# Where the row loads of the second and third expert pair are requested in a routed MoE on one core

## The chip, the cores and the metric

One core of one Trainium2 chip runs the whole program. The metric is the device time of one execution in microseconds (us). The kernel before took 1014.53 us in the median of 3 runs (1013.32 to 1015.21).

## The reference, cut to what matters

Two layers (DEPTH = 2) follow one another. Each mixes the tokens, attends to a memory, and ends with a mixture of experts on 256 tokens of width 1024. The experts' part is what the change touches:

```python
g_logits = t @ w_rg                       # 4 groups; the best one is taken
e_in = e_logits of that group             # its 4 experts; the best two are taken
e_w = softmax(top 2 of e_in) * g_w
...
hg = einsum('nd,edf->nef', t, w_gate)     # 16 experts, 1024 -> 512
hu = einsum('nd,edf->nef', t, w_up)
act = silu(hg) * hu * gates
y = einsum('nef,efd->nd', act, w_down)    # 512 -> 1024
```

So each token goes to two of sixteen experts.

## The kernel before, in words

All is float32. Each engine has a program of its own, written out by hand, and semaphores tie them together.

**Weights.** SyncE (SP) requests all weight units of 2 MB in halves of 1 MB (L520), in a fixed order, into a ring of 7 slots and some buffers that have become free (one more in the first layer, three in the second). Before it requests a unit it waits until its slot's tenant has been read. For expert units this is the semaphore slots_read, which ScalarE (ACT) counts up: it waits for TensorE's count r_jobs and then adds one (units_read, L1336 to L1339). For the first pair of experts there are counts named half (the first half of gate's two units has been read), gate, up, and one at the end of the pair. The last pair's up and down units come in quarters (L561), the two experts' quarters in turn.

**Sorting tokens.** The router gives each token two slots of a table by_slot in HBM (64 rows for each of 16 experts). GpSimd (POOL) sends the normalised tokens there with four indirect transfers (L1498); their landing is counted by r_sent. The first pair's rows do not come from the table: TensorE gathers them on the chip (L975) and starts at once. The rows of pair p from 1 on are loaded back from by_slot by ACT, 512 KB for each pair, with load_rows(p) (L1334), into one of two halves of the buffer rot. For pairs 1 and 2 these two requests stand in ACT's program behind the first exponential of pair 0 (L1347). From pair 3 on the request stands three pairs ahead.

**One pair of experts on TensorE (PE).** gate_up(p) (L1040) multiplies the rows by gate and then by up; VectorE (DVE) makes silu(gate)*up from ACT's exponential (L2011 to L2017). turned(p) then has two parts: the transposes of that product (L1089), and the transposes of the next pair's rows (rows_transposes, L1064), which wait for r_loaded of those rows. In the first layer's pair 0 the rows' transposes come first (rows_first, L179). In the second layer's pair 0 they come after the product's. Behind both stand the gate weights' transposes (L1097), the down product (L1110), and, in the first layer's pairs 0 to 4, a piece of the next layer's keys and values (L628, L630), for which ACT requests 2 MB units (L1252) on its own queue. The results are added back to the tokens by to_tokens (L1071) and DVE (L1993).

The order on ACT around the change is that of the code: wait for half, add to slots_read; wait for gate, add to slots_read; wait for r_sent; exponential; two requests; wait for up, add to slots_read; and so on.

Of the kernel before, what the change touches and what calls it, by code (L numbers as in the profile page):

```python
# [19 lines left out]
M = T // P  # L20
# [194 lines left out]
def trunk(nc, x_in, mem_in, pos_in, inv_in, gains_in, og_in, w_mix, w_router, w_experts, nf_in, out):  # L215
    ctx = ExitStack()
    with ctx:
# [117 lines left out]
        def per_layer(name):  # L335
            return [sem(f"{name}{l}") for l in range(DEPTH)]
# [20 lines left out]
        r_sent = per_layer("r_sent")  # L357
# [822 lines left out]
        def _(act):  # L1180
# [48 lines left out]
            for L in range(DEPTH):  # L1229
# [24 lines left out]
                def next_kv(j, b):  # L1254
                    empty_kv(L + 1, j, b)
                    if j % 2 and j < 7:
                        load_kv((j + 1) // 2)
# [75 lines left out]
                def load_rows(p):  # L1333
                    act.dma_start(rows[p % 2], by_slot[p * P:(p + 1) * P, :]).then_inc(r_loaded[L][p % 2], 16)  # L1334

                def units_read(p, name):  # L1336

                    act.wait_ge(r_jobs[L], ROUTED[L][p, name])
                    act.sem_inc(slots_read, 1)  # L1339

                def routed(p):
                    if p == 0:
                        units_read(p, "half")
                    units_read(p, "gate")
                    if p == 0:
                        act.wait_ge(r_sent[L], 16 * 2 * M)
                    nc.scalar.activation(rexp_of[L], banks[2][:, :], ACT.Exp, scale=-1.0).then_inc(r_gexp[L], 1)  # L1347
                    if p == 0:
                        for q in (1, 2):
                            load_rows(q)  # L1350
                    units_read(p, "up")
                    for half in range(2):
                        act.wait_ge(r_jobs[L], ROUTED[L][p, f"act{half}"])
                        nc.scalar.activation(ractT_of[L][:, 2 * half:2 * half + 2, :], banks[ACT_BANK[half]][:, 0:2 * P].rearrange("p (c t) -> p c t", c=2),
                                             ACT.Copy).then_inc(r_evac[L], 1)
                    act.wait_ge(r_jobs[L], ROUTED[L][p, "weights"])
                    nc.scalar.activation(gatedT, banks[7][:, 0:M * P].rearrange("p (m t) -> p m t", m=M), ACT.Copy).then_inc(r_evac[L], 1)
                    if p + 3 < PAIRS:
                        load_rows(p + 3)
                    for n in range(2):  # L1360
                        act.wait_ge(r_jobs[L], ROUTED[L][p, f"down{n}"])
                        nc.scalar.activation(yrows[:, n * W:(n + 1) * W], banks[5 + n][:, :], ACT.Copy).then_inc(r_evac[L], 1)  # L1362
                    act.sem_inc(slots_read, 1)
                    if L + 1 < DEPTH and ROUTER_KV + p < LOOP_KV:
                        next_kv(ROUTER_KV + p, banks[0])
# [13 lines left out]
                def dense_last():  # L1379
                    if L + 1 < DEPTH:  # L1380
                        for j in range(ROUTER_KV, LOOP_KV):
                            next_kv(j, banks[j])

                either_way(act, L, routed, dense, None, None, None, dense_last)

            squares_of_sums(DEPTH - 1)
# [732 lines left out]
```

## Time and profile before

| what | value |
|---|---|
| median of 3 runs | 1014.53 us |
| the profiled execution | 1015.3 us |
| its span, first to last instruction | 1013.4 us |
| its mean granted TensorE clock | 0.993 |
| PE busy | 988.4 us, 98% |
| DVE busy | 485.1 us, 48% |
| ACT busy | 136.5 us, 13% |
| POOL busy | 98.4 us, 10% |
| loads of ring slots by SP | 64.9% of 16 DMA engines' span |

Times in the profile count from the first instruction; the execution is 1.9 us longer than the span. In the lists of instructions the columns are: start (us), duration (us), engine, line, operation, output<-inputs, count of merged instructions, and in brackets the idle time of the engine before it and what ended it. An engine name with a q is its sequencer, which issues DMAs. The first layer's expert part lies at about 305 to 555 us, the second layer's at about 790 to 1006 us.

### The profile page before, as it was taken

What the parts mean: (1) busy time and instruction counts of PE and PEld (TensorE: products, weight loads), DVE (VectorE), ACT (ScalarE), POOL (GpSimd) and SP (SyncE); (2) the same over time, 40 slices, a digit from 0 to 9 for tenths busy, and PEclk for the clock granted to TensorE, in tenths of its full rate; (3) what the DMA queues carried; (4) which work ended last, traced back from release to release, by engine and by line L of the source; (5) the groups of instructions that cost most, each with busy time, mean ns of one, the idle gap of its engine ahead of it and who ended that gap; (6) DMA issues with size and microseconds to landing.
All of it is one profiled execution on the core that took longest, in us unless ns stands there. A gap on an engine that the chain in (4) does not pass through costs nothing.

```text
span 1013.4 us, 11694 instructions
## 1 busy us (share of the span) xinstructions
PE 988.4 (98%) x4744; PEld 532.2 (53%) x4744; DVE 485.1 (48%) x845; ACT 136.5 (13%) x323; POOL 98.4 (10%) x123
## 2 busy tenths in 40 slices
PE   8999999999998999999999999999999899999996
PEld 7658445669574453333333854465974333333332
DVE  2534386766554224422444636776656434444334
ACT  3211001412011010101112000041020101111111
POOL 3051032000020000000000513210000100000000
PEclk9999999999999999999999999999999999999999
DMA  9973101864289999999999420077385899999995
GB/s 356 425 310 122 45 1 48 372 249 163 88 309 377 397 424 419 420 423 420 421 422 420 180 84 1 1 288 284 133 316 210 340 403 421 420 420 421 420 417 200
DMA packets 44828, 293.61 MB, mean 290 GB/s; under 512 B 5472, under 2 KB 5728, under 8 KB 13024
## 3 DMA queue, kind: packets, MB, share of 16 engines
q1 hardware_dynamic: 38000, 266.36, 64.9%
q10 hardware_dynamic: 5616, 22.24, 5.6%
q0 software_dynamic: 1152, 4.19, 1.1%
q8 instruction: 40, 0.66, 0.3%
q14 instruction: 20, 0.16, 0.0%
HBM read 283.33 MB, written 9.44 MB: 289 GB/s over the span
## 4 chain that ended last, share of the span: by engine, by line
PE 94%; DMA 2%; DVE 2%; POOL 1%; issue 1%; ACT 0%; POOLq 0%; DVEq 0%; ACTq 0%
PE bank L1040 20%; PE bank L1110 11%; PE bank L598 8%; PE bank L1071 6%; PE bank L628 6%; PE bank L813 6%; PE bank L630 5%; PE bank L608 5%; PE bank L867 5%; PE bank L931 5%; PE bank L701 5%; PE bank L588 2%; DMA rot<-by_slot 2%; PE bank L901 1%; PE bank L885 1%; PE bank L1064 1%
## 5 line engine op out<-in xcount | busy, mean ns | idle before, releaser
L1040 PE MATMUL bank<-ring,hT 128*64 128x512 f32 x704 | 195.0, 593 | 0.0
L1040 PEld LDWEIGHTS bank<-ring,hT 128*64 128x64 f32 x704 | 62.3, 137 | 87.4 <-issue 87.4
L598 PE MATMUL bank<-ring,hT 128*128 128x512 f32 x192 | 85.6, 599 | 0.0
L1993 DVE TENSOR_TENSOR x<-bank,x 128x512 f32<-128x512 f32 x64 | 44.3, 692 | 51.1 <-PE bank L1071 51.1
L2011 DVE TENSOR_SCALAR xs<-xs 128x512 f32<-128x512 f32 x8 | 3.4, 427 | 124.2 <-ACT xs L1347 124.1
L1071 PE MATMUL bank<-PT 128*128 128x512 f32 x128 | 59.2, 605 | 0.0
L1110 PE MATMUL bank<-ring,Vx 128*64 128x512 f32 x160 | 57.9, 603 | 0.0
L598 PEld LDWEIGHTS bank<-ring,hT 128*128 128x128 f32 x192 | 35.5, 190 | 40.7 <-issue 40.2
L1110 PE MATMUL bank<-ring,xs 128*64 128x512 f32 x224 | 56.7, 595 | 0.0
L608 PE MATMUL bank<-hT,ring 128*128 128x256 f32 x256 | 55.7, 379 | 0.8 <-DVE hT L1622 0.8
L813 PE MATMUL bank<-ring,hT 128*128 128x512 f32 x128 | 56.3, 595 | 0.1
L608 PEld LDWEIGHTS bank<-hT,ring 128*128 128x128 f32 x256 | 48.6, 190 | 8.0 <-issue 1.4
L1040 PE MATMUL bank<-work,hT 128*64 128x512 f32 x112 | 49.3, 593 | 0.0
L1415 POOL TENSOR_TENSOR sm<-sm 128x1 f32<-128x1 f32 x4 | 1.0, 242 | 462.8 <-ACT rot L1225 462.8
L1071 PEld LDWEIGHTS bank<-PT 128*128 128x128 f32 x128 | 23.0, 189 | 35.9 <-issue 34.2
L813 PEld LDWEIGHTS bank<-ring,hT 128*128 128x128 f32 x128 | 23.8, 190 | 28.6 <-issue 28.1
L2011 DVE TENSOR_SCALAR Vx<-Vx 128x512 f32<-128x512 f32 x8 | 3.4, 427 | 72.7 <-ACT Vx L1347 72.7
L1622 DVE TENSOR_TENSOR hT<-bank,gains 128x512 f32<-128x512 f32 x24 | 15.4, 685 | 35.5 <-PE bank L588 35.5
L1362 ACT ACTIVATE PT<-bank 128x512 f32<-128x512 f32 x32 | 19.1, 597 | 97.9 <-PE bank L1110 97.9
L1040 PEld LDWEIGHTS bank<-work,hT 128*64 128x64 f32 x112 | 15.2, 137 | 32.0 <-issue 32.0
L1477 POOL TENSOR_TENSOR work<-work 128x256 f32<-128x256 f32 x28 | 20.7, 741 | 115.6 <-PE bank L736 100.7
L1110 PEld LDWEIGHTS bank<-ring,xs 128*64 128x64 f32 x224 | 17.5, 137 | 25.0 <-issue 25.0
(302 smaller groups left out, 1550.0 us busy)
## 6 DMA issues: line engine op xcount, KB each, us to landing
ring<-in_w_experts SPq DMA_DIRECT2D x146, 1024.0 KB, 14.0
ring<-in_w_mix SPq DMA_DIRECT2D x60, 1024.0 KB, 14.1
work<-in_w_experts SPq DMA_DIRECT2D x20, 1024.0 KB, 11.2
late<-in_w_experts SPq DMA_DIRECT2D x10, 1024.0 KB, 13.2
late<-in_w_mix ACTq DMA_DIRECT2D x4, 2048.0 KB, 10.2
keys<-in_w_experts SPq DMA_DIRECT2D x8, 1024.0 KB, 16.4
rot<-by_slot ACTq DMA_DIRECT2D x14, 512.0 KB, 8.0
by_slot<-late ACTq DMA_DIRECT2D x1, 4096.0 KB, 37.9
```

Of the source, the lines that this page charges most:

```text
L598: last = nc.tensor.matmul(b[:, :], lhs[:, c, m * P:(m + 1) * P], w[:, c, :], start=(c == 0), stop=(c == C - 1))
L608: last = nc.tensor.matmul(b[:, k * T:(k + 1) * T], w[:, c, (n2 + k) * P:(n2 + k + 1) * P], rhs[:, c, :], start=(c == 0), stop=(c == C - 1))
L628: last = nc.tensor.matmul(b[:, k * T:(k + 1) * T], w[:, c, n:n + P], memory[:, c, :], start=(c == 0), stop=(c == C - 1))
L630: last = nc.tensor.matmul(b[:, :], memory[:, c, (j % 2) * P:(j % 2 + 1) * P], w[:, c, :], start=(c == 0), stop=(c == C - 1))
L701: last = nc.tensor.matmul(b[:, :], rows_at[:, c, :], weights[:, c, :], start=(c == 0), stop=(c == 3))
L813: last = nc.tensor.matmul(held[name[1:], n, m][:, :], hT[:, c, m * P:(m + 1) * P], w[:, c, :], start=(c == 0), stop=(c == C - 1))
L867: last = nc.tensor.matmul(b[:, n * P:(n + 1) * P], weights[:, c, n * P:(n + 1) * P], rows_at[:, c, :], start=(name not in ONTO and n == 0 ...
L931: last = nc.tensor.matmul(b[:, :], rows_at[:, c, :], weights[:, c, :], start=(name not in ONTO and c == 0), stop=(c == 3), skip_group_chec ...
L1040: last = nc.tensor.matmul(banks[2 + g][b2 * CAP:(b2 + 1) * CAP, :], rows_T_of(p)[:, c, b2 * CAP:(b2 + 1) * CAP], w, start=(c == 0), stop=( ...
L1071: routed_job(nc.tensor.matmul(banks[OUT_BANK[n][m]][:, :], gatedT[:, m, :], yrows[:, n * W:(n + 1) * W], start=True, stop=True))
L1110: last = nc.tensor.matmul(banks[5 + n][b2 * CAP:(b2 + 1) * CAP, :], ractT_of[L][:, c, b2 * CAP:(b2 + 1) * CAP], w, start=(c == 0), stop=(c ...
L1993: V.tensor_tensor(xv, banks[OUT_BANK[n][m]][:, :], xv, ALU.add).then_inc(r_added[L], 1)
```

## The change

In ACT's routed(p), for pair 0 alone, the wait for r_sent and the request for pair 1's rows stand between the count half and the count gate. The request for pair 2's rows stays behind the exponential.

```diff
@@ -1341,13 +1341,12 @@
                 def routed(p):
                     if p == 0:
                         units_read(p, "half")
+                        act.wait_ge(r_sent[L], 16 * 2 * M)
+                        load_rows(1)
                     units_read(p, "gate")
-                    if p == 0:
-                        act.wait_ge(r_sent[L], 16 * 2 * M)
                     nc.scalar.activation(rexp_of[L], banks[2][:, :], ACT.Exp, scale=-1.0).then_inc(r_gexp[L], 1)
                     if p == 0:
-                        for q in (1, 2):
-                            load_rows(q)
+                        load_rows(2)
                     units_read(p, "up")
```

ACT's program in the first layer, from the end of the branch that is not taken to the end of pair 0, before (r_jobs is TensorE's count, r_sent the landing of GpSimd's sends, rot the buffer for rows, xs the exponential's place in this layer; the additions to slots_read are not rows of their own):

```order
L496 UNCONDITIONAL_BRANCH
L1347 ACTIVATE xs<-bank 128x512 [waits r_jobs0,r_sent0]
L1334 DMA rot<-by_slot 128x1024 x2
L1354 ACTIVATE xs<-bank 128x256 [waits r_jobs0] x2
L1357 ACTIVATE PT<-bank 128x256 [waits r_jobs0]
L1334 DMA rot<-by_slot 128x1024
L1362 ACTIVATE PT<-bank 128x512 [waits r_jobs0] x2
```

The same place of the changed kernel, whose lines behind the edit have numbers lower by one:

```order
L496 UNCONDITIONAL_BRANCH
L1334 DMA rot<-by_slot 128x1024 [waits r_jobs0,r_sent0]
L1347 ACTIVATE xs<-bank 128x512 [waits r_jobs0]
L1334 DMA rot<-by_slot 128x1024
L1353 ACTIVATE xs<-bank 128x256 [waits r_jobs0] x2
L1356 ACTIVATE PT<-bank 128x256 [waits r_jobs0]
L1334 DMA rot<-by_slot 128x1024
```

One request has moved ahead of the exponential, and the wait for r_sent has moved with it.

ACT's program in the second layer at the same place (Vx is the exponential's place there), before:

```order
L1347 ACTIVATE Vx<-bank 128x512 [waits r_jobs1,r_sent1]
L1334 DMA rot<-by_slot 128x1024 x2
L1354 ACTIVATE Vx<-bank 128x256 [waits r_jobs1] x2
L1357 ACTIVATE PT<-bank 128x256 [waits r_jobs1]
L1334 DMA rot<-by_slot 128x1024
```

And changed:

```order
L1334 DMA rot<-by_slot 128x1024 [waits r_jobs1,r_sent1]
L1347 ACTIVATE Vx<-bank 128x512 [waits r_jobs1]
L1334 DMA rot<-by_slot 128x1024
L1353 ACTIVATE Vx<-bank 128x256 [waits r_jobs1] x2
L1356 ACTIVATE PT<-bank 128x256 [waits r_jobs1]
```

The move is the same one. No instruction of PE, DVE, POOL or SP has moved.

## Rows read from the trace of the kernel before

**Rows 1.** The page: busy times, and the shares of the chain.

```profile
PE 988.4 (98%) x4744; PEld 532.2 (53%) x4744; DVE 485.1 (48%) x845; ACT 136.5 (13%) x323; POOL 98.4 (10%) x123
...
PE 94%; DMA 2%; DVE 2%; POOL 1%; issue 1%; ACT 0%; POOLq 0%; DVEq 0%; ACTq 0%
```

**Rows 2.** The chain of waits, first layer: start us, us, what.

```profile
306.91 7.10 PE bank L1040 x32
...
314.15 9.22 DMA rot<-by_slot
...
323.41 1.09 PE bank L1064 x8
324.50 0.44 PE bank L1089 x4
...
325.20 7.09 PE bank L1110 x32
332.28 7.10 PE bank L628 x32
```

**Rows 3.** The list of instructions in order of time, first layer.

```profile
302.14 0.95 POOL L1498 DMA_INDIRECT by_slot<-xs,wsm  x1 [0.31 <-issue]
...
314.12 0.60 ACT L1347 ACTIVATE xs<-bank 128x512 f32<-128x512 f32 x1 [8.37 <-PE bank L1040]
314.15 1.01 ACTq L1334 DMA_DIRECT2D rot<-by_slot  x2
...
320.97 0.76 DVE L2017 TENSOR_TENSOR xs<-bank,xs 128x256 f32<-128x256 f32 x2 [1.16 <-PE bank L1040]
...
323.41 1.09 PE L1064 MATMUL bank<-ident,rot 128*128 128x128 f32 x8 [2.55 <-DMA rot<-by_slot]
```

**Rows 4.** The line L520 from 310 to 312 us, then L1334 from 310 to 316 us.

```profile
L520 SPq DMA_DIRECT2D ring<-in_w_experts x2: 328/906/1484, 310.6 to 311.0; - x2
...
L1334 ACTq DMA_DIRECT2D rot<-by_slot x2: 347/490/632, 314.1 to 314.5; - x2
...
DMA to landing us min/median/max: 9.2/10.9/12.6
```

**Rows 5.** The chain of waits, second layer.

```profile
793.51 8.04 DMA by_slot<-xs,wsm
...
801.59 7.87 DMA rot<-by_slot
...
811.89 8.23 PE bank L1110 x32
```

**Rows 6.** The list of instructions in order of time, second layer.

```profile
795.20 0.45 SPq L520 DMA_DIRECT2D ring<-in_w_experts  x1
798.26 0.33 SPq L520 DMA_DIRECT2D late<-in_w_experts  x1
801.58 0.60 ACT L1347 ACTIVATE Vx<-bank 128x512 f32<-128x512 f32 x1 [14.06 <-DMA by_slot<-xs,wsm]
801.59 0.82 ACTq L1334 DMA_DIRECT2D rot<-by_slot  x2
...
807.34 1.02 PE L1089 MATMUL bank<-ident,Vx 128*128 128x128 f32 x4 [2.30 <-DVE Vx L2017]
809.50 1.97 PE L1064 MATMUL bank<-ident,rot 128*128 128x128 f32 x8 [1.14 <-DMA rot<-by_slot]
```

**Rows 7.** Landings on SP's queue: L520 issued 794 to 797 us, then L561 from 983.5.

```profile
DMA to landing us min/median/max: 7.0/8.1/9.1
...
DMA to landing us min/median/max: 15.6/15.6/15.7
```

**Rows 8.** Stretches: PE, PEld, DVE, ACT, POOL busy, granted clock, DMA share, GB/s.

```profile
799.00:802.00 3.00, 3.00 (x18) 1.00 (x16) 0.00 (x0) 0.42 (x1) 0.00 (x0) 1.00 1.01 422
808.00:811.00 3.00, 1.86 (x9) 1.51 (x8) 0.35 (x1) 0.73 (x2) 0.00 (x0) 0.50 1.01 421
811.00:814.30 3.30, 3.30 (x11) 1.25 (x11) 2.55 (x8) 0.38 (x1) 0.00 (x0) 0.50 1.03 425
820.00:823.00 3.00, 3.00 (x18) 0.98 (x16) 0.00 (x0) 0.60 (x1) 0.00 (x0) 1.00 0.95 333
321.00:324.00 3.00, 0.59 (x5) 0.59 (x6) 0.73 (x2) 0.00 (x0) 0.00 (x0) 1.00 1.03 427
```

**Rows 9.** The end: the last request of weights, and the chain there.

```profile
983.96 1.07 SPq L561 DMA_DIRECT2D ring<-in_w_experts  x1
...
995.50 7.07 PE bank L1110 x32
```

**Rows 10.** DMA issues of the page: KB each, median us from issue to landing.

```profile
rot<-by_slot ACTq DMA_DIRECT2D x14, 512.0 KB, 8.0
...
work<-in_mem SPq DMA_DIRECT2D x2, 512.0 KB, 3.8
```

## The prediction

> **What bounds the kernel now.** I read the page first, to see which engine has no room. PE is busy for 98% of the span and makes up 94% of the chain that ended last [rows 1]. So a change that adds no work to PE can only win back PE's idle time, or cost by adding some. I then followed the chain of waits through both expert parts, since the edit acts only in pair 0 of each layer. The reader is to see one piece in the first layer that is no work at all: 9.22 us of a load of rows, between gate_up and the transposes of those rows [rows 2]. The list of instructions gives what it costs: 2.55 us of idle PE ahead of L1064 [rows 3]. Most of the 9.22 us are hidden by the up product. In the second layer the chain runs over the sends to by_slot (8.04 us) and then the load of rows (7.87 us) [rows 5], and PE idles twice: 2.30 us ahead of L1089, ended by DVE, and 1.14 us ahead of L1064, ended by the rows [rows 6]. The stretches and SP's landings come last. They say whether the weight stream has room, and that bounds what the second layer can give.
>
> **First layer: the request moves forward.** It is issued at 314.15 now, just after the exponential [rows 3]. In the changed kernel ACT issues it when half has been counted and the sends have landed.
>
> - Half: SP's two requests at 310.6 and 311.0 are what this count releases [rows 4], so it falls at 310.6.
> - Sends: the trace does not show their landing here. The last is issued at 302.14 [rows 3]. With the second layer's 8.04 us [rows 5] it lands at 310.2. The exponential at 314.12 waited for PE, not for the sends [rows 3], so 314.1 is the upper bound, and there the request would gain nothing. I take 310.2: those 8.04 us were measured beside two weight loads, here there is only one other load.
>
> The request then goes out at 310.7, 3.45 us earlier. Its time to land is not known for that moment. Near rows: 9.2 us for the same load at 314.15 and 12.6 us for the one queued behind it [rows 4], 3.8 us for a load of this size with little beside it [rows 10]. A 2 MB load of the next layer's weights stands ahead of it on ACT's queue, so a value above 3.8 us is right. I take 9.2 us, the same load 3.5 us later. It lands at 319.9. The bounds are 314.5 and 323.3.
>
> PE finishes gate_up at 323.41 - 2.55 = 320.86 [rows 3]. With rows at 319.9 the wait is gone. What is late next? The transposes of rows take 1.09 us [rows 2], to 321.95. The product's transposes need L2017, which ends at 320.97 + 0.76 = 321.73 [rows 3]. It is ready just in time, so nothing takes the wait's place. **Term 1: -2.5 us**, from 0 (sends late) over -0.1 (12.6 us) to -2.55. The exponential still starts when gate is done, the count gate is not held back, and SP's requests stay where they are. Behind this the chain is PE alone (down, then keys and values [rows 2]), with no DMA piece until the second layer's sends, so the 2.5 us carry through.
>
> **Second layer: nothing is requested earlier, and a count is held back.** Half releases SP's two requests that end at 795.20; gate releases those from 798.26 on [rows 6]. The sends land only at 801.55 [rows 5]. So the request cannot go before 801.6, where it is now. Three small things move.
>
> - The exponential starts behind one request instead of beside it. Two requests take 0.82 us [rows 6], one about 0.4. DVE's three steps and L1089 move by 0.4, so the first idle time becomes 2.7 us and L1089 ends at 808.36 + 0.4 = 808.75 (808.36 is 809.50 - 1.14 [rows 6]).
> - The count gate comes at about 802.0 instead of 798.2. SP's two second halves are requested 3.8 us later. I price this below.
> - Pair 1's rows are now requested ahead of those 2 MB instead of behind them. They took 7.87 us behind a full queue [rows 5] and 3.8 us is the other end [rows 10]. The first halves are still landing until 795.2 + 9.1 = 804.3 [rows 7]. Being between, I take 5.9 us, landing at 807.5. Then PE goes on at 808.75 instead of 809.50. **Term 2: -0.7 us**, from +0 (7.87 us again, still 809.5) to -1.14 (all of that idle time), and a little more if the clock stays up (below).
>
> **The weight stream.** The DMA engines run full from 799 on [rows 8] and end late: the last request at 983.96 lands 15.7 us later, at 999.7 [rows 7, 9]. The down product starts at 995.50 and takes 7.07 us for four quarters [rows 9], so its last quarter starts at 995.50 + 3 x 1.77 = 1000.8. The slack is 1.1 us. Term 2 uses 0.7 of it. Do the held-back halves use the rest? The first halves keep the engines busy until 804.3, and requests at 802.0 and 802.4, plus the rows' 512 KB, fill the queue behind them. If data needed the quick 7.0 us [rows 7] of the same request to land from 802.0, it would be 809.0, where an unbroken stream gives 804.3 + 2.5 (1 MB at 421 GB/s [rows 8]) = 806.8. That is a slip of 2.2 us at most. The rows' 1.2 us of traffic move ahead into that gap, which leaves 1.0. And at 820 to 823 the engines moved 333 instead of 421 GB/s [rows 8], 0.6 us of spare room that a late stream fills. **Term 3: 0 us**, up to +0.4.
>
> **The clock.** In the second layer the granted clock is 0.50 (1.2 GHz) from 808 to 814.3 after PE's idle 2.30 us [rows 6, 8], and L1110 takes 8.23 instead of 7.09 us [rows 2, 5]. In the first layer 2.55 us of idle left it at 1.00 [rows 3, 8]. The Trainium skill, page "TensorE: Matmul & The Clock Gate", section "HAM oscillation", says that waits for DMA between bursts of matmuls throttle PE again and the next burst starts cold. By that rule an idle time grown to 2.7 us speaks against the change, and removing the first layer's 2.55 us gives nothing back. The trace agrees in the second layer only. The sum keeps the clock as it is; the other outcome is a rival.
>
> **Sum.** -2.5 - 0.7 + 0 = -3.2 us. On the profiled execution that is 1015.3 - 3.2 = 1012.1. That execution is 0.8 above the median of 1014.53, so for the median I say **1011.3**. A measurement of this kernel can tell about 0.2%, 2.0 us, from no change.
>
> **Rivals.**
>
> - *A. The first layer gains, the second does not.* Rows in the second layer again need 7.87 us, or the slip takes up the slack. For it: the load there is requested at the same time as before. Against: 2 MB fewer stand ahead of it. -2.5 us, 1012.0.
> - *B. The wait is hidden anyway, or the request is not early.* The sends of the first layer land near 314, or the rows queue behind ACT's own 2 MB load for 12.6 us. The change then does not do what it says. For it: 12.6 us is a real landing of a load that stood second on this queue. Against: that load and the one ahead of it both met SP's loads. Term 1 is -0.1, with term 2 -0.8: 1013.7.
> - *C. The second layer's stream slips in full.* The 3.8 us of delay reach the end, and 1.1 are slack: +2.7, while term 2 is lost. -2.5 + 2.7 = +0.2, 1014.7. For it: from 799 on the engines are full and the slack is thin. Against: the engines still have work at 802.
> - *D. Slower by the clock.* The longer idle time ahead of L1089 keeps the clock at 0.50 through all of pair 0's down product. Sixteen steps at half clock take 2 x 7.09 = 14.2 us instead of 8.23: +6.0 against -3.2 is +2.8, 1017.3. It decides from the point where more than 5.2 us of matmul work that now runs at full clock run at half. Against: PE is dense from 811.9 on, and there the clock came back after 2.4 us.
>
> **How the numbers follow.** Forecast, both terms: 0.62. A: 0.17. B: 0.06. C: 0.08. D: 0.04. The opposite of D, the clock staying up (about -1.5 more, capped by the stream's slack): 0.03. Faster by over 0.2% (below 1012.5) are the forecast, A and the last, 0.82, less 0.03 for A's upper part: 0.79. Within 0.2%: B, C and that part, 0.17. Slower: 0.04. The low end of the range is both idle times won and some of the clock: -2.55 - 1.14 - 1.0 = -4.7, 1009.8. The high end takes in A and most of B: 1013.7.
>
> **What would show it.** Right: in the first layer L1334 is issued near 310.7 and once more behind the exponential, and L1064 starts within 0.1 us of the end of L1040, with no idle time put down to rot. All later starts of the first layer are 2.5 us earlier. In the second layer SP's requests of 798.26 stand near 802, the exponential 0.4 us later relative to the end of the sends, and the idle ahead of L1064 is gone. The last quarter's matmuls do not wait for the ring. Wrong: idle time ahead of L1064 in the first layer over 0.5 us (term 1), a gap in L1110 at the very end (term 3), or a granted clock of 0.50 past the middle of L1110 (D).

## The result, and the profile after

The changed kernel takes 1009.38 us in the median of 5 runs (1009.15 to 1009.99), the kernel before 1014.53 us beside it (5 runs, 1013.32 to 1015.89). The ratio is 0.995, 95% interval 0.9936 to 0.9965: 5.1 us faster, 3.6 to 6.5. The forecast was 1011.3 in 1009.8 to 1013.7. The direction was right, the size was not, and the result lies 0.4 us below the range.

The page of the changed kernel, as [rows 1]:

```profile
PE 984.9 (98%) x4744; PEld 529.3 (53%) x4744; DVE 485.1 (48%) x845; ACT 136.5 (14%) x323; POOL 98.5 (10%) x123
...
PE 86%; SPq 5%; DMA 4%; DVE 2%; POOL 1%; issue 1%; ACT 0%; POOLq 0%; DVEq 0%; ACTq 0%
```

PE is 3.5 us less busy, though it has the same instructions: less of its work ran at half clock. And the chain that ended last now holds 5% of SP's queue and 4% of DMA, with PE down from 94% to 86%; before it held 2% of DMA and nothing of SP's queue.

The first layer in order of time (start, duration, engine, line), as [rows 3]; and the chain there, as [rows 2]:

```profile
309.67 0.35 ACTq L1334 DMA_DIRECT2D rot<-by_slot  x1
313.10 0.60 ACT L1347 ACTIVATE xs<-bank 128x512 f32<-128x512 f32 x1 [8.37 <-PE bank L1040]
313.12 0.34 ACTq L1334 DMA_DIRECT2D rot<-by_slot  x1
```

```profile
305.88 13.96 PE bank L1040 x64
319.84 1.02 PE bank L1064 x8
320.86 0.44 PE bank L1089 x4
321.30 0.22 PE bank L1097 x2
...
321.55 7.09 PE bank L1110 x32
```

The request has moved ahead of the exponential, and the piece of 9.22 us has left the chain. From the start of gate_up to the start of the down product it is 321.55 - 305.88 = 15.67 us, where it was 325.20 - 306.91 = 18.29 [rows 2]: 2.6 us less. gate_up itself began 1.0 us earlier in this execution, ahead of anything that the change touches. That differs from execution to execution: gate_up ends there between 319.8 and 321.4 us in the traces, with no order by kernel.

The second layer, as [rows 6], and the chain there, as [rows 5]:

```profile
790.44 0.46 SPq L520 DMA_DIRECT2D ring<-in_w_experts  x1
...
796.90 0.34 ACTq L1334 DMA_DIRECT2D rot<-by_slot  x1
797.32 0.33 SPq L520 DMA_DIRECT2D late<-in_w_experts  x1
797.37 0.60 ACT L1347 ACTIVATE Vx<-bank 128x512 f32<-128x512 f32 x1 [13.49 <-DMA by_slot<-xs,wsm]
797.38 0.71 ACTq L1334 DMA_DIRECT2D rot<-by_slot  x1
...
803.13 0.77 PE L1089 MATMUL bank<-ident,Vx 128*128 128x128 f32 x4 [2.85 <-DVE Vx L2016]
```

```profile
788.76 8.12 DMA by_slot<-xs,wsm
...
803.13 0.77 PE bank L1089 x4
803.89 0.87 PE bank L1064 x8
804.77 0.22 PE bank L1097 x2
804.99 7.02 PE bank L1110 x32
```

Rows of pair 1 are requested 0.42 us ahead of SP's second halves. L1064 no longer waits, and L1110 takes 7.02 us instead of 8.23. The stretches after, as [rows 8]:

```profile
781.00:786.00 5.00, 4.65 (x32) 3.12 (x31) 3.79 (x23) 1.22 (x6) 1.07 (x1) 1.00 0.61 252
...
803.00:806.00 3.00, 2.87 (x20) 1.98 (x22) 2.03 (x6) 1.09 (x3) 0.00 (x0) 1.00 1.03 427
806.00:812.00 6.00, 6.00 (x30) 2.01 (x28) 1.18 (x5) 0.60 (x1) 0.00 (x0) 1.00 1.00 419
```

The granted clock (the column before the DMA share) stays at 1.00. In the profiled execution of before it was 0.50 (1.2 GHz) from 808 to 814.3 [rows 8]. And it had fallen once more there, ahead of anything that the edit touches in this layer, in the router's part, which the prediction overlooked. The same columns for before:

```profile
780.00:785.00 5.00, 3.59 (x46) 3.32 (x47) 4.14 (x16) 1.15 (x2) 0.74 (x2) 0.86 1.00 421
785.00:790.00 5.00, 5.00 (x27) 3.16 (x26) 3.07 (x21) 1.23 (x6) 0.37 (x1) 0.80 0.55 233
```

Means of 0.86 and 0.80 over 5 us each are 3.4 us at half clock. The four sends come 1.1 us earlier behind L1216 where the clock stays up (12.33 us in the changed kernel, 12.34 with the edit in the second layer alone, 13.43 in before).

The end of the chain, as [rows 9]:

```profile
964.40 0.04 issue
964.45 5.36 PE bank L1110 x22
969.81 3.63 PE bank L1071 x8
973.44 13.91 PE bank L1040 x64
...
988.91 7.75 PE bank L1110 x32
```

The piece ahead of this is a load of ring, 26.05 us from 938.35. Two down products wait for weights:

```profile
964.45 0.64 PE L1110 MATMUL bank<-ring,Vx 128*64 128x512 f32 x1 [0.47 <-DMA ring<-in_w_experts]
```

This one is in pair 6, whose down product lasts from 961.19 to 969.81, 8.62 us, where before needed 7.09; the idle 0.47 us are only part of the 1.5. Pair 7's takes 7.75 us instead of 7.07. At the end of pair 0's down product (812.01 against 820.12) the changed kernel was 8.1 us ahead, at the end of the last down product (996.66 against 1002.57) only 5.9. The weight stream took 2.2 us back.

The 8.1 us are not all the change's doing. 1.0 us is the earlier gate_up of the first layer and 1.1 the clock in the router's part, neither of which the edit touches. 2.6 are the first layer's wait. The other 3.4 lie between the last send and the end of pair 0's down product in the second layer (26.6 us before, 23.25 after); only 0.6 of them are waits (2.30 + 1.14 before, 2.85 after), the rest is work that ran at half clock in this execution of before.

### The profile page after: what moved, and what is told of

Its sections match the earlier page's. It is cut to its first block, busy times and chain, and to the rows that moved or that the text cites. A ratio compares the mean times of both kernels' runs of the same rounds, so it can differ in the third digit from the quotient of the medians.

```text
span 1007.5 us, 11694 instructions
## 1 busy us (share of the span) xinstructions
PE 984.9 (98%) x4744; PEld 529.3 (53%) x4744; DVE 485.1 (48%) x845; ACT 136.5 (14%) x323; POOL 98.5 (10%) x123
## 4 chain that ended last, share of the span: by engine, by line
PE 86%; SPq 5%; DMA 4%; DVE 2%; POOL 1%; issue 1%; ACT 0%; POOLq 0%; DVEq 0%; ACTq 0%
PE bank L1040 16%; PE bank L1110 10%; PE bank L598 8%; PE bank L628 6%; PE bank L813 6%; PE bank L630 6%; PE bank L608 6%; PE bank L867 5%; PE bank L931 5%; PE bank L701 5%; SPq L520 5%; PE bank L1071 5%; DMA ring<-in_w_experts 3%; PE bank L588 2%; PE bank L901 1%; PE bank L885 1%
## 5 line engine op out<-in xcount | busy, mean ns | idle before, releaser
L1110 PE MATMUL bank<-ring,Vx 128*64 128x512 f32 x160 | 57.1, 596 | 0.5 <-DMA ring<-in_w_experts 0.5
L1110 PE MATMUL bank<-ring,xs 128*64 128x512 f32 x224 | 56.7, 595 | 0.0
L1110 PEld LDWEIGHTS bank<-ring,xs 128*64 128x64 f32 x224 | 17.5, 137 | 25.0 <-issue 25.0
```

The costliest lines, as they stand in the source:

```text
L1110: last = nc.tensor.matmul(banks[5 + n][b2 * CAP:(b2 + 1) * CAP, :], ractT_of[L][:, c, b2 * CAP:(b2 + 1) * CAP], w, start=(c == 0), stop=(c ...
```

## The experiments

Each kernel is compared with the kernel before, run beside it on the same chip. Before took 1015.64 us beside the first four, 1016.21 beside the next four (from the repeated changed kernel on) and 1014.52 beside the last four (those with `warm`).

### The edit in one layer alone

In the first layer alone (and the other way round for the second):

```diff
                     if p == 0:
                         units_read(p, "half")
+                    if p == 0 and L == 0:
+                        act.wait_ge(r_sent[L], 16 * 2 * M)
+                        load_rows(1)
                     units_read(p, "gate")
...
-                        for q in (1, 2):
+                        for q in (1, 2) if L != 0 else (2,):
```

Expected of the first layer alone: 

> The edit in the first layer alone. Theory 1 (the first layer's wait of 2.55 us is the main gain, and the end of the kernel is set by the second layer's weight stream): the idle time ahead of L1064 in the first layer is gone, pair 0's down product starts 3.6 us after the end of gate_up less 2.6 us of waiting, and the whole is 2.6 us faster than before, 2 to 3.5. Theory 2 (most of the 5 us come from the second layer's edit): also 2.6 us here, but then the second layer alone must give 2 or more. Theory 3 (the rest is the clock, which falls at other places when the first layer's 2.6 us shift the second layer): 4 us or more here.

Measured: 1009.99 against 1015.64 us, ratio 0.9948 (0.9931 to 0.9966), 5.3 us by the ratio. The wait is gone and the down product starts 15.67 us after gate_up, as in the changed kernel. That is 2.6 us; the other 2.7 are not in the wait. Theory 1 (2 to 3.5) is too small, and 5.3 us is in theory 3's range; which clock it would be, this run doesn't say.

Expected of the second layer alone: 

> The edit in the second layer alone. Theory 1: 0.7 to 1.5 us faster, since TensorE gains some 0.8 us or more at L1064 but the last weights' landing lets through only about 1.1 us. Theory 2: 2 to 3 us faster. Theory 3: within 1 us of before, and which stretches run at half clock differs from run to run. In all, the rows of pair 1 land 5 to 6 us after their request instead of 7.9.

Measured: 1013.41 us, ratio 0.9982 (0.9967 to 0.9996), 1.8 us. So the second layer's edit counts too. The interval, 0.4 to 3.3 us, reaches from theory 1 into theory 2; theory 2 falls by the run above, where the first layer alone gave 5.3 us and not 2.6. The rows landed 4.0 us after their request, sooner than the 5 to 6 expected. The two gains together (0.70%) are not told apart from what both edits give at once (0.50%, and 0.63% in a second measurement).

### What the held-back count costs

```diff
                         units_read(p, "half")
+                        act.wait_ge(r_sent[L], 16 * 2 * M)
                     units_read(p, "gate")
-                    if p == 0:
-                        act.wait_ge(r_sent[L], 16 * 2 * M)
```

> Only the wait for the sends is moved ahead of the count gate; both requests for rows stay behind the exponential. It shows what the held-back count costs by itself. Theory 1: SP's second halves in the second layer go out 3.8 us later, the engines have work till then, and the time stays within 0.5 us of before. Rival (the stream slips): 1 to 2.7 us slower, and the last weights land that much later.

Measured: 1014.44 us, ratio 0.9986 (0.9975 to 0.9998). The delay is there (the second halves go out 6.8 us after the first, 3.4 more than before) and costs nothing that can be seen; the slip of 1 to 2.7 us is ruled out. Why it should even be a little faster is open. The list of instructions of this kernel shows the order in the second layer:

```profile
799.40 0.33 SPq L520 DMA_DIRECT2D late<-in_w_experts  x1
799.45 0.60 ACT L1346 ACTIVATE Vx<-bank 128x512 f32<-128x512 f32 x1 [13.04 <-DMA by_slot<-xs,wsm]
799.47 0.83 ACTq L1334 DMA_DIRECT2D rot<-by_slot  x2
...
DMA to landing us min/median/max: 8.2/9.9/11.6
```

The last line is that of the two requests for rows. The request for pair 1's rows comes 0.07 us behind SP's, and lands after 8.2 us. With the edit in the second layer alone it goes out first:

```profile
800.01 0.34 ACTq L1334 DMA_DIRECT2D rot<-by_slot  x1
800.43 0.33 SPq L520 DMA_DIRECT2D late<-in_w_experts  x1
...
DMA to landing us min/median/max: 4.0/6.3/8.6
```

0.42 us ahead of SP's request the same load lands after 4.0 us. In both traces SP's first halves were requested 6.4 to 6.5 us before the rows, so it is not their age that differs. All traces agree: where the rows' request goes out ahead of SP's second halves (six traces) they land after 4.0 to 5.2 us, where it goes out behind them (eight traces) after 7.8 to 8.4. Holding back the count helps only as far as it lets the rows go first. One thing is not separated: where the rows go first, pair 2's request follows 0.5 us later and behind SP's, otherwise at once.

### Is TensorE or the weight stream the end of the changed kernel?

```diff
                     turned(p)
+                    if L + 1 == DEPTH and p == 1:
+                        for _ in range(2):
+                            nc.tensor.matmul(banks[5][:, :], ident[:, :], xs[:, 0, 0:W], start=True, stop=True)
                     down(p)
```

> The changed kernel with two more matmuls of 128x512 float32 (0.86 us each, 1.7 us in all) on TensorE in the second layer's pair 1, into a bank that is overwritten later. Theory 1 (the second layer of the changed kernel ends with its weight stream, TensorE has some 2 us to spare): 0 to 0.4 us slower than the changed kernel, 4.7 to 5.1 us faster than before. Rival (TensorE's own work sets the end): 1.7 us slower than the changed kernel, 3.4 us faster than before.

Measured: 1011.59 us, ratio 0.9959 (0.9943 to 0.9974). That is 4.2 us faster than before and 0.9 us slower than the changed kernel by the first measurement of that (0.995), 2.2 by the second. The interval, 2.6 to 5.8 us faster than before, holds the rival's 3.4 us and theory 1's 4.7 alike, so the times alone don't decide. In its trace the last down product takes 7.08 us and waits for nothing. In the profile of the changed kernel the waits for weights add up to 1.5 + 0.7 = 2.2 us, so there TensorE had 2.2 us to spare. But the traces differ in more than the added 1.7 us: in this one the clock was at half for 3.4 us in pair 0, in the changed kernel's it was not. The second profile of the changed kernel, below, has the same fall, and only its last down product waits (7.65 us, 0.6 too many). So the spare time is about 2 us when the clock stays up, 0.6 when it falls, and the added 1.7 us use up most or all of it.

The changed kernel once more, beside the three that follow: 

> The changed kernel once more, beside the next three. It should again be 4 to 6 us faster than before, in a narrow band of 1 us, with its time independent of the mean granted clock of an execution.

Measured: 1009.9 against 1016.21 us, ratio 0.9937 (0.9924 to 0.9951). The band was 2 us wide (1009.54 to 1011.6). The two highest of its six had a mean clock of 0.995, the others 0.997 or 0.998, so its time isn't independent of the clock. In the first measurement it had looked so: five runs with mean clocks from 0.994 to 0.998, within 0.9 us of each other and in no order by clock.

### The clock behind the first layer's wait

Each run has its mean granted clock on record. The kernel before, the 37 runs beside the first eight kernels (at 0.990 and at 0.996 there was one each):

| mean clock | runs | median us |
|---|---|---|
| 0.995 | 4 | 1014.4 |
| 0.994 | 5 | 1014.5 |
| 0.993 | 18 | 1016.0 |
| 0.991 | 8 | 1017.6 |

A clock that is down by 0.004 over 1013 us is 8 us at half speed, in which densely busy TensorE loses 4 us; the medians differ by 3.2. The profiled execution (1015.3 us, 0.993) did not show the clock falling in the first layer. A fourth theory was that in other executions it does. The test keeps the wait and fills it:

```diff
                     def next_rows():
+                        if L + 1 < DEPTH and p == 0:
+                            for _ in range(2):
+                                nc.tensor.matmul(banks[5][:, :], ident[:, :], hT[:, 0:2, :], start=True, stop=True)
```

> The kernel before, with two matmuls of 128x512 float32 (1.7 us) on TensorE in the first layer's idle time of 2.3 to 2.55 us ahead of L1064; the rows' request and landing stay as they are. Theory 4 (in many executions of before, though not in the profiled one, that idle time also lets the granted clock fall to 0.5 in dense matmul work behind it, which the change takes away with the wait): 1.5 to 2.5 us faster than before, the high executions above 1016 nearly gone, the mean granted clock up from 0.993 to 0.995, and L1064 still starts when the rows land. Theory 1 (only the wait itself counts): same as before within 0.5 us.

Measured: 1013.14 us, ratio 0.9969 (0.9956 to 0.9982), 3.1 us faster with two useless matmuls more; no run above 1014.71; mean clock 0.996. Its list of instructions shows that the rows still decide:

```profile
321.32 1.98 PE L1079 MATMUL bank<-hT,ident 128*128 128x512 f32 x4
323.52 1.09 PE L1064 MATMUL bank<-ident,rot 128*128 128x128 f32 x8 [0.22 <-DMA rot<-by_slot]
```

L1064 starts 2.1 us after the end of gate_up, a little sooner than in the kernels that wait there without filling (2.2 to 2.55 us in four traces). 3.1 us for the clock and 2.6 for the wait make 5.7, what the edit in the first layer alone gave in medians (1015.64 - 1009.99 = 5.65). But 3.1 us (1.8 to 4.5) need not all be the clock right behind this wait: the mean clock rose by 0.003, some 6.5 us at half, and this profile also lacks the fall in the second layer's router part. The last four kernels separate the two.

### Another order in the second layer

```diff
                         units_read(p, "half")
-                        act.wait_ge(r_sent[L], 16 * 2 * M)
-                        load_rows(1)
+                    if p == 0 and L + 1 < DEPTH:
+                        act.wait_ge(r_sent[L], 16 * 2 * M)
+                        load_rows(1)
                     units_read(p, "gate")
                     nc.scalar.activation(rexp_of[L], banks[2][:, :], ACT.Exp, scale=-1.0).then_inc(r_gexp[L], 1)
+                    if p == 0 and L + 1 == DEPTH:
+                        act.wait_ge(r_sent[L], 16 * 2 * M)
+                        load_rows(1)
```

> The first layer as in the changed kernel; in the second layer the counts half and gate and the exponential come first, and only then the wait for the sends and both requests. If the weight stream sets the end of the changed kernel and the held-back count costs it 0.8 us (the last weights landed at 993.85 with the edit in the first layer alone and at 994.68 with both): 0.5 to 1 us faster than the changed kernel, last landing 0.8 us earlier, and SP's second halves requested 3.5 us after the first. If TensorE sets the end: the same as the changed kernel or up to 0.7 us slower, since the rows land 7.9 us after the request again.

Measured: 1011.32 us, ratio 0.9955 (0.9941 to 0.9969), 1.4 us above the 1009.9 of the changed kernel beside it. Neither outcome that was named came; the intervals overlap, but nothing is gained. The chain in the second layer:

```profile
796.37 0.03 ACT Vx L1348
796.39 8.39 DMA rot<-by_slot
...
804.82 1.09 PE bank L1064 x8
```

SP's second half goes out at 796.32 there, 0.07 us ahead of the rows, and the rows need 8.39 us. PE idles only 0.60 us ahead of L1089 and 0.35 ahead of L1064 there, less than the changed kernel's 2.85. But in this execution the clock was at half for 6.8 us in the router's part, ahead of the experts, so its trace can't tell what the order costs.

### The clock in the second layer

The changed kernel with two matmuls of 128x512 ahead of L1089 in the second layer's pair 0:

```diff
                         next_rows()
+                    if L + 1 == DEPTH and p == 0:
+                        for _ in range(2):
+                            nc.tensor.matmul(banks[5][:, :], ident[:, :], xs[:, 0, 0:W], start=True, stop=True)
                     if p:
```

> The changed kernel, with two matmuls (1.7 us) in the second layer's idle time of 2.8 us ahead of L1089. If the clock in the second layer costs time in the changed kernel: 0.5 to 1.2 us faster than it. If the weight stream takes up what the clock costs there: the same within 0.3 us, with the mean granted clock higher.

Measured: 1010.22 us, ratio 0.994 (0.9926 to 0.9955), the same as the changed kernel's 1009.9; mean clock 0.9977 against 0.9967. That is the second outcome: the clock is higher and the time is not shorter.

For the next four, three matmuls of 128x256 were added to the router's part of the second layer too, ahead of its waits:

```diff
                 p_seventh("p_3", range(3, 4))
+                def warm(w):
+                    if L + 1 == DEPTH:
+                        wait_emptied(pe, L, "p_2")
+                        nc.tensor.matmul(banks[BANK["router_kv0"]][:, 0:w], ident[:, :], hT[:, 0:w // P, 0:P], start=True, stop=True)
+                warm(2 * P)
...
                 router_kv(0, range(1, 2))
+                warm(2 * P)
                 logits(1)
...
                 router_kv(0, range(2, 6))
+                warm(2 * P)
                 pe.wait_ge(normed, 6 * L + 5)
```

The changed kernel with both fillings: 

> The changed kernel with matmuls that have no use in TensorE's waits of the second layer: three of 128x256 in the router's part and two of 128x512 ahead of L1089. The clock should stay at 1.00 there (mean 0.998 or more). Theory 4 (in the changed kernel only the clock in the router's part still costs time; the rest is taken up by the weight stream): 0.3 to 1 us faster than the changed kernel and no execution above 1010.5.

Measured: 1009.23 us (1008.93 to 1009.73), ratio 0.9947 (0.9933 to 0.9961), mean clock 0.9986. By the ratio this lies between the two measurements of the changed kernel (0.995 and 0.9937), so the filling shows no gain; the changed kernel itself was not run beside it.

The kernel before with these, the two matmuls ahead of L1089 and the first layer's filling: 

> The kernel before with the same, and two matmuls in the first layer's wait for rows. With the clock up everywhere only the waits themselves are left between this and the changed kernel with the same filling: theory 4 says that this one is 2.6 us slower than that, up to 3.5 with what TensorE gains in the second layer, and mean clock 0.998. Theory 1 says the same of the waits, but that this kernel is no faster than before; theory 4 that it is 4 to 5 us faster than the median of before.

Measured: 1011.38 us (1010.73 to 1013.26), ratio 0.9969 (0.9958 to 0.998), mean clock 0.9984. Only waits are left between this and the one above: 2.15 us, with the slowest run of the one above (1009.73) below the fastest of this one. Both forecasts of theory 4 were too high: 2.6 to 3.5 us for the waits, and 4 to 5 us ahead of before, where 3.1 came. Theory 1, no faster than before, is out.

The same without the first layer's filling (the three added lines of `next_rows` above): 

> The kernel before with the second layer filled, but not the first layer's wait for rows. Against the kernel before with all filled, this is the price of the clock behind the first layer's wait alone. Theory 4: 1.5 to 3 us slower than with all filled, with a wide band, and mean clock 0.996. Theory 1: the same.

Measured: 1013.0 us (1010.54 to 1015.74), ratio 0.9982 (0.9971 to 0.9993), mean clock 0.9969. The first layer's filling is worth 1.6 us here (3.1 in the test above, where the second layer was not filled). The single runs show that it is the clock: three of the eleven had a mean clock of 0.999 and took 1010.5 to 1012.1 us, like the six of the filled kernel at 0.998 or 0.999 (1010.7 to 1011.7). The other eight had 0.994 to 0.997 and took 1012.8 to 1015.7. And here the profiled execution was one in which the clock fell. Its stretches in the first layer, and its chain:

```profile
320.00:323.00 3.00, 0.83 (x6) 0.47 (x5) 0.75 (x2) 0.00 (x0) 0.00 (x0) 1.00 1.02 425
323.00:326.00 3.00, 3.00 (x16) 1.96 (x16) 2.40 (x6) 1.15 (x3) 0.00 (x0) 0.59 1.02 426
326.00:329.00 3.00, 3.00 (x14) 0.90 (x12) 0.50 (x2) 0.00 (x0) 0.00 (x0) 0.84 1.00 423
```

```profile
313.65 8.84 DMA rot<-by_slot
...
323.62 0.78 PE bank L1102 x4
...
324.83 8.10 PE bank L1123 x32
```

L1123 is the down product, 8.10 us instead of 7.09. This is the part of the wait's price that the profile of before did not show [rows 8].

The other order in the second layer (its diff stands above), with `warm` in the router's part: 

> The edit in the first layer; in the second one the counts and the exponential ahead of the wait for the sends; the router's part filled as above. If the held-back count costs the weight stream 0.6 to 0.8 us and the stream sets the end: 0.5 to 0.9 us faster than the changed kernel with filling, near 1008.4. If the earlier result of this order (1011.3, slower than the changed kernel) was the order's doing and not that of the half clock that stood in the router's part of its profile: 1 us or more slower than the changed kernel with filling.

Measured: 1011.3 us (1009.88 to 1011.75), ratio 0.9963 (0.9949 to 0.9976), 2.1 us above the changed kernel with filling. So the order is slow also without the half clock in the router's part. PE waits 3.07 us for the rows, so that the idle time which the early exponential saves ahead of L1089 (0.60 us instead of 2.85) comes back ahead of L1064, and the clock falls behind that:

```profile
801.58 0.77 PE L1099 MATMUL bank<-ident,Vx 128*128 128x128 f32 x4 [0.60 <-DVE Vx L2030]
805.42 1.97 PE L1074 MATMUL bank<-ident,rot 128*128 128x128 f32 x8 [3.07 <-DMA rot<-by_slot]
```

```profile
803.00:806.00 3.00, 0.58 (x3) 0.59 (x4) 0.00 (x0) 0.00 (x0) 0.00 (x0) 0.59 1.00 416
806.00:809.00 3.00, 3.00 (x13) 1.94 (x13) 2.27 (x6) 0.38 (x1) 0.00 (x0) 0.50 1.03 423
```

None of these kernels is faster than the changed one by more than the measurement can tell.

## Why the prediction was right or wrong

**The first layer's wait, term 1: right.** The request went out at 309.67 (310.7 was forecast, and gate_up began 1.0 us earlier in this execution), the rows landed 7.2 us later (9.2 were taken, the same load in a fuller queue), well ahead of the end of gate_up at 319.8. The product's transposes followed without a gap, as said. 2.5 us were forecast, 2.6 came. The sends' unseen landing did no harm: the request stood right behind the count half, as its mates on SP's queue did. Rival B is out.

**The clock: the step that failed.** "The sum keeps the clock as it is" took one execution for all. There the idle 2.55 us left the clock at 1.00 [rows 3, 8], and I read that as "removing it gives nothing back". The runs showed in its place that the clock does fall behind that wait in part of the executions. Filling the wait gave 1.6 us where the second layer's clock was held up, and 3.1 where it was not, of which some may lie elsewhere. One trace shows the clock falling to half there, at 323.6. The same idle time has this price in some executions and not in others. By the rule of the Trainium skill, page "TensorE: Matmul & The Clock Gate", section "HAM oscillation" (waits for DMA between bursts throttle PE), taking a wait away gives clock back; the prediction's sentence that by this rule it gives nothing back had it the wrong way round. The page's example has longer waits; that waits of 2.2 to 2.55 us do it in some executions is what these runs add. The runs shown before held a hint: they were 1.9 us apart while the wait itself is nearly constant (2.2 to 2.55 us in four traces). The opposite of D, the clock staying up, was named, but only for the second layer and with a chance of 0.03; in the profiled execution of the changed kernel it came.

**Term 2, the second layer: right in its mechanism, too small by about 1 us.** The request was not earlier against the sends, the exponential came 0.5 us later (0.4 forecast), the idle time ahead of L1089 grew to 2.85 (2.7) and the one ahead of L1064 went. The rows landed after 5.2 us (5.9). The sum took only the 0.7 us at L1064, and 0.6 us less idle time is what came (2.30 + 1.14 against 2.85). The edit alone gave 1.8 us, 0.4 to 3.3, so the forecast lies inside; how much of that is clock was not separated.

**Term 3, the weight stream: right.** SP's second halves went out 7.25 us after the first ones (790.07, 797.32), where it had been 3.4. Holding the count back costs nothing to be seen. And the stream's slack did cap the second layer: the chain ends over a load, and 2.2 us were taken back. That cap may also be why the changed kernel's runs lie so close together; it was not tested. Rival C is out.

**Rival D** did not come: the longer idle time of 2.85 us left the clock at 1.00 in the profiled execution. In the second profile of the changed kernel it was at half for 3.4 us behind an idle time of 2.73.

With the clock held up in the second layer's waits, then in the first layer's too, then with the edit in place of the first layer's filling, the medians are 1013.0, 1011.38 and 1009.23 us, from 1014.52 for the kernel before beside them. Of these 5.3 us, 2.15 are waits and 3.15 are clock, half of that (1.6) behind the very wait that was removed. The other 1.5 are the clock in the second layer, router part included, and there it was the filling that held it up, not the edit. That the edit alone gives as much (5.1 and 6.3 us) fits with the fillings adding nothing to the changed kernel; where it wins the second layer's 1.5 us was not separated.

## What to carry to other kernels

Price a wait of TensorE at its idle time and at the matmuls behind it that may run at half clock, and take the second part from many executions' mean clock, not from one trace; filling the wait with useless matmuls measures it without moving the wait. Where a small load that is needed soon shares the DMA engines with a stream of large ones, request it just ahead of the stream's next pieces, even if they have to be held back for it. Then look at what ends the kernel: here a stream with 1.1 us of slack took back 2.2 us of what was won ahead of it.

## What the runs showed of the hardware that was not expected

- 0.5 us in the order of two requests on different queues go with 4 us of landing. A 512 KB load requested 0.42 us ahead of a 1 MB load on SP's queue landed after 4.0 to 5.2 us in six traces. Requested 0.07 us behind it, after 8.2 and 8.4 us, and 3.3 us behind it, after 7.9 (before).
- Idle times of TensorE of 2.2 to 3.1 us were followed by a fall of the clock to half in some executions and not in others, with the same kernel too (the changed kernel: 2.85 us without, 2.73 with), and 2.85 us left it up where 2.17 us brought it down.
- Two useless matmuls in a wait made the kernel before 3.1 us faster (1.8 to 4.5).
